# A two-layer transformer pair on one core: the last output projection by Strassen's seven products of halves, in two units, with three products as filling among the last heads

## The reference, cut to what matters

```python
def odd_mixer(h, w_in, w_out, cos, sin):
    proj = jnp.einsum('bsd,de->bse', h, w_in)
    q, k, v, z = jnp.split(proj, _offsets(ODD_SIZES), axis=-1)
    o = moba_attention(q, k, v, cos, sin) * jax.nn.silu(z)
    return jnp.einsum('bse,ed->bsd', o, w_out)      # w_out: 1024 x 1024
...
    x = x + gate[:, None, :] * y
return rms_norm(x, final_g)
```

## Time and profile before

| | |
|---|---|
| median of 3 executions | 1539.21 us (1538.62 to 1539.52) |
| the profiled execution | 1540.88 us, span in the trace 1539.1 us |
| last fillings begin / last product ends / trace ends | 1500.77 / 1531.0 / 1539.1 us |
| busy over the span | PE 99%, PEld 87%, DVE 67%, ACT 28% |
| granted clock of PE, mean | 0.997 |

### The profile page before, as it was taken

The page is one execution under the profiler, slowest core; times in us unless marked ns, Lnnn a source line. Parts: engine busy times, 40 slices in busy tenths (PEclk is TensorE's granted clock), DMA queues, the critical chain, the costliest instruction groups (busy, mean ns, idle before and its releaser), DMA issues.

```text
span 1539.1 us, 27693 instructions
## 1 busy us (share of the span) xinstructions
PE 1517.8 (99%) x11127; PEld 1345.9 (87%) x11127; DVE 1035.6 (67%) x1942; ACT 431.3 (28%) x925; POOL 12.6 (1%) x26
## 2 busy tenths in 40 slices
PE   8999999999999999999999999999999999999998
PEld 7998869898899999899878899799999787678887
DVE  5788886477667774678897367667765565535663
ACT  5415424012100001335423211200011455424432
POOL 1000000000000000100000000000000000000000
PEclk9999999999999999999999999999999999999999
DMA  8543443363465444344242442485544745553320
GB/s 277 185 165 111 149 153 111 112 203 124 154 231 166 158 172 168 132 163 145 97 165 94 154 165 83 137 274 168 169 165 158 266 143 217 219 183 122 135 109 28
DMA packets 172385, 243.40 MB, mean 158 GB/s; under 512 B 16830, under 2 KB 95332, under 8 KB 172260
## 3 DMA queue, kind: packets, MB, share of 16 engines
q1 hardware_dynamic: 170372, 237.96, 44.9%
q10 hardware_dynamic: 1888, 3.67, 0.7%
HBM read 240.56 MB, written 1.05 MB: 157 GB/s over the span
## 4 chain that ended last, share of the span: by engine, by line
PE 94%; DVE 4%; ACT 1%; issue 1%; DMA 0%; SPq 0%; DVEq 0%; POOL 0%; ACTq 0%
PE psum L630 34%; PE psum L1647 27%; PE psum L1502 6%; PE psum L1302 3%; PE psum L3115 3%; PE psum L445 2%; PE psum L1561 2%; PE psum L1297 2%; PE psum L3207 2%; PE psum L428 1%; PE psum L1431 1%; PE psum L3215 1%; PE psum L461 1%; PE psum L1403 1%; PE psum L1342 1%; PE psum L664 1%
## 5 line engine op out<-in xcount | busy, mean ns | idle before, releaser
L630 PE MATMUL psum<-hT,ring 128*128 128x256 f32 x1552 | 342.8, 380 | 1.1 <-ACT hT L3312 0.7
L630 PEld LDWEIGHTS psum<-hT,ring 128*128 128x128 f32 x1552 | 292.3, 190 | 45.5 <-issue 7.1
L630 PE MATMUL psum<-uT,ring 128*128 128x256 f32 x384 | 84.9, 380 | 0.0
L1647 PE MATMUL psum<-hT,ring 128*128 128x128 f32 x704 | 82.4, 275 | 1.0 <-issue 1.0
L630 PEld LDWEIGHTS psum<-uT,ring 128*128 128x128 f32 x384 | 72.6, 190 | 10.4 <-DVE uT L1165 0.6
L1647 PEld LDWEIGHTS psum<-hT,ring 128*128 128x128 f32 x704 | 80.4, 192 | 1.5 <-issue 1.5
L1928 ACT ACTIVATE SCR<-SCR 128x512 f32<-128x512 f32 x22 | 13.9, 630 | 219.6 <-DVEq L2713 219.6
L512 DVE TENSOR_TENSOR psum<-psum,const 128x512 f32<-128x512 f32 (+4 forms) x41 | 22.1, 558 | 62.0 <-PE psum L445 61.3
L491 ACT ACTIVATE SCR<-psum,stats 128x128 f32<-128x128 f32 (+2 forms) x128 | 49.9, 406 | 26.1 <-DVE stats L526 25.3
L1647 PE MATMUL psum<-G,ring 128*128 128x128 f32 x400 | 47.8, 276 | 0.0
L477 ACT ACTIVATE SCR<-psum 128x512 f32<-128x512 f32 (+2 forms) x60 | 26.3, 497 | 73.4 <-PE psum L461 73.4
(11 more groups left out here) (656 smaller groups left out, 3006.9 us busy)
## 6 DMA issues: line engine op xcount, KB each, us to landing
ring<-in_w_in SPq DMA_DIRECT2D x46, 1024.0 KB, 6.8
ring<-in_ffn_w_gate_up SPq DMA_DIRECT2D x88, 512.0 KB, 5.7
ring<-in_w_ada SPq DMA_DIRECT2D x24, 1024.0 KB, 8.8
ring<-in_ffn_w_down SPq DMA_DIRECT2D x16, 1024.0 KB, 5.6
ring<-in_w_in_odd SPq DMA_DIRECT2D x16, 1024.0 KB, 7.3
ring<-in_w_in_even SPq DMA_DIRECT2D x10, 1024.0 KB, 7.2
ring<-in_x_w_kv SPq DMA_DIRECT2D x8, 1024.0 KB, 6.0
ring<-in_ssm_w_glu SPq DMA_DIRECT2D x8, 1024.0 KB, 5.4
```

The lines of the kernel that those rows point to most:

```text
L630: ins = nc.tensor.matmul(b[0:width, n * S:n * S + S], w[k // 4][:, k % 4, c0[n]:c0[n] + width], tile(k), start=k == 0, stop=k == kt - 1)
L1647: ins = nc.tensor.matmul(banks[job][:, at:at + P], left, right, start=first, stop=last)
```

## The change

The output projection becomes two units of seven products, unit u for the output channels 512u to 512u+511. Each product is 8 matmuls of 128 columns instead of matmuls of 256 columns. Products 1 and 5 of unit 0 are the filling of step 8, product 1 of unit 1 that of step 9, and the other 11 follow the last head in the order of `OUT_LATE`. DVE makes 4 sums of weights for each unit and 4 differences of gated tokens, and adds each product of a unit to the residual by itself, in pieces of 128 x 128, as often as Strassen's formula has it. ACT copies product 1 of each unit from PSUM first, and squares the residual in other groups.

```diff
-          8: ["part 0", "part 1"], 9: ["part 2"]}
+          8: ["part 0 1", "part 0 5"], 9: ["part 1 1"]}
...
+OUT_JOBS = [(0, "a"), (1, "a"), (0, "b"), (0, "c"), (0, "d"), (1, "b"), (1, "c"), (1, "d")]
+OUT_LATE = [(1, 5), (0, 2), (1, 2), (0, 6), (0, 7), (0, 4), (0, 3), (1, 6), (1, 7), (1, 4), (1, 3)]
+OUT_SUMS = [(0, 0), (1, 0), (0, 1), (0, 2), (0, 3), (1, 1), (1, 2), (1, 3)]
...
+        def odd_out(u, p):
...
+            if p in MIXED_OF:
+                pe.wait_ge(sig["tokens_mixed"], 4 + MIXED_OF[p] + 1)
+            if p in SUM_OF:
+                pe.wait_ge(sig["weights_mixed"], 4 * len(SEVENS) + OUT_SUMS.index((u, SUM_OF[p])) + 1)
+            for g in range(2):
+                for k in range(4):
...
+                    at = S * i + P * g
+                    ins = nc.tensor.matmul(b[:, at:at + P], weights, tokens, start=k == 0, stop=k == 3)
...
+        def odd_added(u, m_, n, what, first_of_two=False):
...
+            for g in range(2):
+                k = 4 * u + 2 * g + m_
+                x = xT[:, k, n * P:(n + 1) * P]
+                ins = V.scalar_tensor_tensor(out=x, in0=what[:, g * P:(g + 1) * P], scalar=ada[:, 40 + k:41 + k], in1=x,
+                                             op0=ALU.mult, op1=ALU.add)
...
+            if job == "a":
+                link(odd_added(u, 0, 0, one))
+                jobs.release(odd_added(u, 0, 0, second), name)
+            elif job == "b":
+                link(V.tensor_tensor(two, one, first, ALU.add))
+                jobs.release(V.tensor_tensor(four, two, second, ALU.add), name)
+                jobs.evacuated(dve, name)
+                odd_added(u, 0, 1, four)
+                odd_added(u, 1, 1, four)
+                link(odd_added(u, 1, 0, two))
+            elif job == "c":
+                odd_added(u, 1, 1, first)
+                link(odd_added(u, 1, 0, first))
+                jobs.release(odd_added(u, 1, 0, second), name)
+                jobs.evacuated(dve, name)
+            else:
+                jobs.release(odd_added(u, 0, 1, first, u == 1), name)
+                jobs.evacuated(dve, name)
...
+            if i == 8:
+                odd_weights((0, 0))
+                dve.wait_ge(sig["gated"], 2)
+                for k in (1, 2, 3):
+                    ojobs.evacuated(dve, f"c heads{k}")
+                odd_tokens((0,))
             att_c.dve(nc, dve, link, i, (lambda: twice_silu("c")) if i == 1 + PAIR_LAG + 1 else None)
+            if i == 9:
+                odd_weights((0, 1))
...
+                odd_weights((1, 0))
-        residual("odd out", 1, 8, ODD_TILES, final_gains)
...
+        odd_tokens((1, 2, 3))
+        odd_weights((0, 2), (0, 3))
+        odd_store(0, "a")
+        odd_weights((1, 1))
+        odd_store(0, "b")
+        odd_weights((1, 2))
+        odd_store(0, "c")
+        odd_weights((1, 3))
+        odd_store(0, "d")
+        odd_store(1, "a")
+        final_gains(range(4))
+        odd_store(1, "b")
+        four_squares = [sq[:, 2 * c:2 * c + 2, :] for c in range(2)]
+        dve.wait_ge(sig["squares"], 9)
+        link(V.tensor_tensor(four_squares[0], *four_squares, ALU.add))
+        link(V.tensor_tensor(sq[:, 0, :], sq[:, 0, :], sq[:, 1, :], ALU.add))
+        dve.sem_inc(sig["summed"], 1)
+        odd_store(1, "c")
+        final_gains((5, 7))
+        dve.wait_ge(sig["squares"], 10)
+        for k in (5, 7):
+            link(V.tensor_tensor(sq[:, 0, :], sq[:, 0, :], sq[:, k, :], ALU.add))
+        dve.sem_inc(sig["summed"], 1)
+        odd_store(1, "d")
+        final_gains((4, 6))
```

More of the change, by code:

```diff
@@ L2815, in second_plan @@
     names += pair_jobs(C_UNITS, C_FILL)
-    names += [f"odd out{c}" for c in range(5)] + [f"final{n}" for n in range(4)]
+    names += [f"O{u} {job}" for u, job in OUT_JOBS] + [f"final{n}" for n in range(4)]
     return names
@@ L2952, in second_block @@
                              for i in range(4))
+    odd_sums = [[QKr[:, 1024 * i:1024 * i + 1024].rearrange("p (k g n) -> p k g n", g=2, n=P) for i in range(4)], sums]
     a_out = m["kx"]
@@ L3122, in even_tile @@
             pe.wait_ge(sig["gated"], 1) if k < 4 else ojobs.evacuated(pe, f"b heads{k - 4}")
+        def odd_out(u, p):
+            job = next(x for x, made in PRODUCTS.items() if p in made)
+            i, name = PRODUCTS[job].index(p), f"O{u} {job}"
+            first = p in (1, 5) or job in "cd" and i == 0
+            if first:
+                out_banks[name] = jobs.begin(pe, name, early=p in (1, 5))
+            b = out_banks[name]
+            w = [ring.arrived(pe, f"odd out{u}.{h}") for h in range(2)]
+            if p in MIXED_OF:
[4 more added lines that the diff above has]
+                for k in range(4):
+                    if p in TOKENS_OF:
+                        half, n = TOKENS_OF[p]
+                        if g == 0:
+                            odd_tile(4 * half + k)
+                        tokens = z[:, 4 * half + k, n * P:(n + 1) * P]
+                    else:
+                        tokens = mixed[MIXED_OF[p]][:, k, :]
+                    if p in WEIGHTS_OF:
+                        m_, half = WEIGHTS_OF[p]
+                        weights = w[half][:, k, 256 * g + P * m_:256 * g + P * m_ + P]
+                    else:
+                        weights = odd_sums[u][SUM_OF[p]][:, k, g, :]
+                    at = S * i + P * g
+                    ins = nc.tensor.matmul(b[:, at:at + P], weights, tokens, start=k == 0, stop=k == 3)
+            if p in (2, 6, 4, 3):
+                close(ins)
         def odd_tile(k):
@@ L3241, in final @@
             for i in range(4):
-                pe.wait_ge(sig["gained_out"], (1, 1, 2, 2, 3, 3, 4, 5)[4 * half + i])
+                pe.wait_ge(sig["gained_out"], (1, 1, 1, 1, 3, 2, 3, 2)[4 * half + i])
                 ins = nc.tensor.transpose(b[:, i * P:(i + 1) * P], hT[:, 4 * half + i, t * P:(t + 1) * P], ident)
             close(ins)
-        for c, c0 in zip((3, 4), pair(3)):
-            transposed(f"odd out{c}", wide("odd out1"), (c0,), z, KT, (P,))
+        for u, p in OUT_LATE:
+            odd_out(u, p)
         final(0)
@@ L3293, in square @@
             warm()
-            for c, tiles in enumerate(EVEN_TILES if n == 2 else ODD_TILES):
-                jobs.evacuated(act, f"{'even' if n == 2 else 'odd'} out{c}")
-                nc.scalar.activation(sq[:, tiles, :], xT[:, tiles, :], ACT.Square).then_inc(sig["squares"], 1)
+            if n == 2:
+                for c, tiles in enumerate(EVEN_TILES):
+                    jobs.evacuated(act, f"even out{c}")
+                    nc.scalar.activation(sq[:, tiles, :], xT[:, tiles, :], ACT.Square).then_inc(sig["squares"], 1)
+            else:
+                for u in range(2):
+                    b = jobs.full(act, f"O{u} a")
+                    if u:
+                        jobs.evacuated(act, "O0 b")
+                    else:
+                        jobs.evacuated(act, f"{SEVENS[-1]} b")
+                    nc.scalar.activation(one, b[:, 0:S], ACT.Copy).then_inc(sig["parts_copied"], 1)
+                for job, tiles in (("O0 d", slice(0, 4)), ("O1 c", slice(5, 8, 2)), (None, slice(4, 5)),
+                                   ("O1 d", slice(6, 7))):
+                    if job:
+                        jobs.evacuated(act, job)
+                    else:
+                        act.wait_ge(sig["out_added"], 1)
+                    nc.scalar.activation(sq[:, tiles, :], xT[:, tiles, :], ACT.Square).then_inc(sig["squares"], 1)
             b = ojobs.full(act, f"square {n}")
@@ L3461, in modulated, with final_gains, residual @@
             scaled(lambda k: gains[:, k:k + 1], hT, sig["scaled"], r)
-        def final_gains(c):
-            jobs.evacuated(dve, f"odd out{c}")
-            for k in range(ODD_TILES[c].start, ODD_TILES[c].stop):
+        def final_gains(tiles):
+            for k in tiles:
                 ins = V.tensor_scalar(hT[:, k, :], xT[:, k, :], col("final", k), None, ALU.mult)
             ins.then_inc(sig["gained_out"], 1)
-        def residual(prefix, layer, before, all_tiles, after=None):
+        def residual(prefix, layer, before, all_tiles):
             for c, tiles in enumerate(all_tiles):
@@ L3661, in seven_store, with odd_weights @@
                 mix_weights(u + 1, (3,))
+        def odd_weights(*which):
+            for u, i in which:
+                w = [ring.arrived(dve, f"odd out{u}.{h}").rearrange("p k (g m n) -> p k g m n", g=2, m=2)
+                     for h in range(2)]
+                q = [[w[half][:, :, :, m_, :] for half in range(2)] for m_ in range(2)]
+                made = odd_sums[u]
+                x, y, op = ((q[1][0], q[1][1], ALU.add), (made[0], q[0][0], ALU.subtract),
+                            (q[0][0], q[1][0], ALU.subtract), (q[0][1], made[1], ALU.subtract))[i]
+                link(V.tensor_tensor(made[i], x, y, op))
+                dve.sem_inc(sig["weights_mixed"], 1)
@@ new lines, in odd_tokens @@
+        def odd_tokens(which):
```

(10 more changed lines are left out.)

32 lines of the change are left out of this document (17 added, 15 removed).

## The result

The change made the kernel slower: 1545.67 us (median of 5 executions, 1545.09 to 1545.86) against 1539.52 us for the kernel before (5 executions, 1538.62 to 1539.78). The ratio is 1.0039, with a 95% interval of 1.0027 to 1.0051, that is 4.2 to 7.9 us. The profiled execution took 1545.45 us, with a span of 1543.3 us. Medians in this document leave out one of run 4's twelve executions, which took 1573.74 us at a granted clock of 0.946.

What follows compares the result with a forecast made beforehand. PE bounds the kernel before, but DVE sets the changed kernel's end: last squares 5.0 us later plus 0.3 us for PE's lower clock give 5.3 us more, a median of 1544.5 us, 0.34% slower, range 1541.3 to 1547.8.

Steps and rivals of the forecast that it cites:

- PE is shorter by 2.9 us: Output projection on PE: 14 products of 1.79 us, 25.06 us, replace 27.98 us of matmuls, 2.9 us less.
- Step 8's sum and difference are covered, and the last store is 4.8 us earlier: Ahead of the last head: DVE's added work is covered by 1.5 and 0.3 us; last pair's store ends 4.8 us earlier.
- An update at 128 columns steps 0.27 us: DVE's 36 residual updates: 0.27 us a step, 0.345 for a burst's last, bounds 0.20 and 0.41, 10.6 us in all.
- DVE's list takes 27.2 us: DVE behind the last head's store: work laid end to end from 1509.40, last residual update ending at 1536.62 against 1531.69.
- PE stands 1.2 us for the bank of job a: Unit 1's product 3: PE asks at 1526.3 for a bank DVE releases at 1527.4, so it stands 1.2 us.
- The lower clock costs 0 to 0.4, taken as 0.3: PE's sum of squares after a rest of 6 us: 0 to 0.4 us more at the lower clock, taken as 0.3.
- The tail: End of the kernel: 6.96 us from the end of the last square to the trace's end, taken as unchanged.
- PE is not the bound: Answers the rival that PE stays the bound through the projection: 2.9 us earlier, 1536.3 us; 2 in 100.
- the updates do cost more than plain sums: Answers the rival that DVE's small updates are as cheap as plain sums: 1542.0 or 1540.5 us; 13 in 100.
- they do gain from being half as wide: Answers the rival that DVE's updates gain nothing from half the width: 5 us more, 1549.5 us; 6 in 100.

Runs made afterwards that it cites:

- run 4: 12 of the 36 updates of the residual left out of the changed kernel: 1540.82 us, ratio 1.0010 to the kernel before.
- run 3: Twelve matmuls of 256 columns added to the changed kernel to fill PE's rest ahead of the sum of squares: 1544.28 us, ratio 1.0030 to the kernel before.
- run 6: Changed kernel with sums of weights earlier, all squares summed by PE and final gains on ACT: 1540.18 us, ratio 1.0006 to the kernel before.
- run 7: Kernel of run 6 with the squares of tiles 0 to 3 added on DVE again: 1537.54 us, ratio 0.9988 to the kernel before.
- run 2: Changed kernel with PE summing the squares of all eight tiles, DVE's four sums of squares gone: 1541.34 us, ratio 1.0013 to the kernel before.
- runs 1 and 5: Each against the changed kernel. 1: unit 0's four sums of weights made in step 7, 1542.90 us; 5: final gains moved from DVE to ACT, 1543.64 us.

## Why the prediction was right

The forecast was 5.3 us more; the trace has 5.1. The mechanism is the one forecast, DVE's list behind the last head's store; that the sum comes so close is in part luck. Point by point:

- **PE is shorter by 2.9 us**: it was 2.5. A product steps 1.79 us as read from the earlier trace rows. But the four products next to the last heads took longer, 1.87 to 1.95 us from start to start (1501.72 to 1503.67 is 1.95), so that both fillings of step 8 took 3.82 us instead of 3.58. It costs nothing, as DVE is later.
- **Step 8's sum and difference are covered, and the last store is 4.8 us earlier**: right. Counted from the first filling the store ends at 8.59 us; before it was 13.40. It was forecast at 8.63.
- **An update at 128 columns steps 0.27 us**: right. A burst of six takes 1.67 us, (1.67 - 0.345) / 5 = 0.265, and run 4 gives 0.28 with what lies around them. The bursts of the 36 add up to 10.5 us (1.67 and 1.77 for the sixes, 0.61 for a pair), where I had 10.6. So a step fell from 0.40 us at 256 columns to 0.265 at half the width, and not by half. The estimate from the Trainium skill, page "VectorE: DVE Perf Modes", section "The TRN2 errata", was 8.3 us, 2.2 too low. The section says itself that its row for operands in SBUF gives too short a time for one instruction, and for the fp32 sum of two tensors it gives one cycle per element and 151 more, an estimate of 291 ns at 128 columns. The trace has 286 ns for that sum and 346 to 349 for the update with its scalar per partition.
- **DVE's list takes 27.2 us**: it took 26.2, so the last update is 3.9 us later than before and not 4.9. The sums up to 1513.85 are right within 0.1 us. What was too dear is the end of a burst: the next sum of weights does not wait for the burst's last write (1515.25 starts ahead of 1514.73 + 0.61), and I had put a hand-over there.
- **PE stands 1.2 us for the bank of job a**: wrong. DVE released it at 1525.68, and PE asked at 1525.84: the list was 0.8 us ahead of my reckoning by then, and PE 0.5 us behind it.
- **The lower clock costs 0 to 0.4, taken as 0.3**: the term that was mis-sized. The root is 1.23 us further behind the last square. 0.8 us of this is the clock (run 3), 0.4 that eight matmuls, for two tiles, stand behind the last square, as the first of these waits for both squares (line 3291 asks for 12 in either case). I had priced the matmuls of one tile, at 0.4 us from half of the row; four of them take 0.58 us at the higher clock in run 3.
- **The tail**: from the root on 6.19 against 6.23 us, right.

The sum came out by two errors that cancel, and that is luck: 1.0 too much for the list, 0.9 too little for PE behind the last square. The rivals fell: PE is not the bound (it rests for 5.45 us, and run 4 shortens DVE alone), the updates do cost more than plain sums (a step of 0.265 us against 0.20), and they do gain from being half as wide (0.265 against 0.40).

What stays open is some 1 us between the difference of the medians, 6.15, and of the traces, 5.1. Some 0.3 us of it lie outside the trace: the five executions of the changed kernel took 2.09 to 2.60 us more than their spans, those of the kernel before in the later comparisons 1.76 to 1.94. Nothing in the stage shows the rest, and the start of the first filling varies more than that from one execution to another.

## What to carry to other kernels

Fewer multiplications for the engine that is the bound of the whole kernel were paid for on the engine that adds the pieces up, and at the end of this kernel that engine became the path: count its instructions by the step that the trace shows for that width, before counting what the first saves. When such work is moved to a third place, ask again which engine is last there; run 6 gave most of its gain away because twenty matmuls of one column fell on an engine that had just become the bound again. A rest as long as here, 4.1 to 5.5 us ahead of the last matmuls, cost a second time by the lower clock: 0.8 us.

## What the runs showed that I had not expected

PE's clock fell in run 6 although PE had no rest. Its windows (stretch, length, PE busy, granted clock, DMA):

```profile
1529.40:1533.20 3.80, 3.80 (x35) 0.92 0.00 0
1533.20:1535.10 1.90, 1.88 (x9) 0.50 0.00 0
```

Ahead of it stood 32 matmuls of a single column, and the transposes behind them took 1.95 us for eight, at 0.50. It cost nothing there, as the time from the root to the end stayed at 6.19 us. In run 7 there were 20 of them, and the same transposes took 1.06 us:

```profile
1526.83 2.63 PE L3293 MATMUL psum<-const,QK 128*128 128x1 f32 x20
1529.61 1.06 PE L3280 MATMUL psum<-const,hT 128*128 128x128 f32 x8
```

Behind the 32 of run 2, with a rest of 1.39 us in their middle, they took 1.80. So PE's clock fell behind 32 matmuls of single columns as it did after the rests of 4.14 to 5.45 us of the changed kernel and of runs 1 and 5, and the sums of squares right behind the rests of 1.39 and 2.04 us in runs 2 and 4 still ran at 1.00. In runs 1 and 5 the fall shows only after the first four matmuls behind the rest: these took 0.58 us, as in run 4, the next eight 1.87.

The first filling, ahead of which the kernels with the change differ in hardly anything, started between 1498.16 and 1500.77 us in the nine profiled executions. In the two earliest (runs 4 and 7) the granted clock between 1200 and 1496 us was 1.00, in the others 0.99. So in these nine an early start goes with the clock far ahead of the change. That a part of the differences between medians is of this kind is likely but not shown; a stage is better compared from its own start.
